# Rotary halves exchanged in the read instead of projected twice, and a retention norm summed with two products per head

## The reference, cut to what matters

```python
def apply_rope(t, cos, sin):                       # 64 channels: halves of 32
    t1, t2 = jnp.split(tf, 2, axis=-1)
    return jnp.concatenate([t1 * cos - t2 * sin, t1 * sin + t2 * cos], axis=-1)

def mla_mixer(h, cos, sin, w_in, q_norm, kv_norm, w_uq, w_ukv, w_o):
    c_q, c_kv, k_r = jnp.split(h @ w_in, [512, 768], axis=-1)      # 512, 256, 64
    q = (rms_norm(c_q, q_norm) @ w_uq).reshape(B, S, 8, 128 + 64)
    q_rope = apply_rope(q[..., 128:], cos, sin)
    kv = (rms_norm(c_kv, kv_norm) @ w_ukv).reshape(B, S, 8, 128 + 128)
    k_rope = apply_rope(k_r, cos, sin)
    ...                                            # causal attention, then @ w_o

def retention_mixer(h, w_in, out_g, w_out):        # 4 heads, keys 256, values 512
    ...
    ret = rms_norm_2(ret, out_g.reshape(4, 512))   # over the 512 values of a head
    y = ret * jax.nn.silu(g)
    return y @ w_out
```

## Time and profile before

| | |
|---|---|
| runs, us | 2784.96, 2791.34, 2791.89; median 2791.34 |
| profiled execution, us | 2785.44 |
| its span on the profile's clock, us | 2783.6 |
| TensorE busy | 2657.9 us, 95% |
| GpSimd busy | 1936.2 us, 70% |
| VectorE busy | 1084.8 us, 39% |
| mean granted TensorE clock | 0.976 of full |

### The profile page before, as it was taken

How to read it: one execution, slowest core, us unless ns; L and a number is a source line. 1 busy time by engine, 2 the same in 40 slices (tenths; PEclk the granted TensorE clock), 3 DMA queues, 4 the chain that set the end, 5 groups by cost and what they waited for, 6 DMA issues and landing times.

```text
span 2783.6 us, 33532 instructions
## 1 busy us (share of the span) xinstructions
PE 2657.9 (95%) x11988; PEld 2124.7 (76%) x11988; DVE 1084.8 (39%) x1871; ACT 735.2 (26%) x1188; POOL 1936.2 (70%) x1664
## 2 busy tenths in 40 slices
PE   6999899998999889999899999999999999899999
PEld 4766788886778668888756788888877877688887
DVE  6323411125666351112437553425531431452424
ACT  3333400113455340011344431202221121421211
POOL 5534688886666478888533388887958757688785
PEclk9999999999999999999989999999999999899999
DMA  5211233222222123223211133333313222233332
GB/s 151 69 38 58 69 101 106 91 94 73 76 60 76 40 82 106 91 93 103 61 46 46 30 91 97 100 92 91 106 47 110 71 74 76 63 104 97 100 91 76
DMA packets 297263, 225.80 MB, mean 81 GB/s; under 512 B 26979, under 2 KB 290124, under 8 KB 297036
## 3 DMA queue, kind: packets, MB, share of 16 engines
q1 hardware_dynamic: 294256, 219.21, 25.9%
q10 hardware_dynamic: 2908, 5.24, 0.5%
HBM read 222.32 MB, written 2.10 MB: 81 GB/s over the span
## 4 chain that ended last, share of the span: by engine, by line
PE 87%; DVE 5%; ACT 2%; issue 2%; POOL 1%; DVEq 1%; DMA 1%; ACTq 0%; SPq 0%; POOLq 0%
PE proj L547 26%; PE proj L549 26%; PE proj L548 26%; PE aux L1933 1%; PE aux L447 1%; PE aux L1853 1%; PE aux L1858 1%; PE aux L1774 1%; ACT L472 1%; POOL w_lo L1158 1%; PE proj L1715 1%; PE aux L1909 1%; PE proj L1714 1%; PE proj L741 1%; POOL w_hi L1153 0%
## 5 line engine op out<-in xcount | busy, mean ns | idle before, releaser
L547 PE MATMUL proj<-a_hi,w_hi 128*128 128x512 f32 x2104 | 841.7, 400 | 47.9 <-DVE a_lo L658 31.6
L549 PE MATMUL proj<-a_hi,w_lo 128*128 128x512 f32 x2104 | 825.1, 392 | 0.0
L548 PE MATMUL proj<-a_lo,w_hi 128*128 128x512 f32 x2104 | 824.6, 392 | 0.0
L1152 POOL TENSOR_TENSOR w_hi<-raw,small 128x512 fp32r<-128x512 f32 x375 | 393.2, 1049 | 593.9 <-PE proj L549 574.5
L1153 POOL TENSOR_TENSOR w_hi<-raw,small 128x512 fp32r<-128x512 f32 (+1 forms) x455 | 490.9, 1079 | 196.2 <-PE proj L549 194.2
L1158 POOL TENSOR_TENSOR w_lo<-raw,w_hi 128x512 fp32r<-128x512 f32 (+1 forms) x455 | 601.0, 1321 | 6.3
L1157 POOL TENSOR_TENSOR w_lo<-raw,w_hi 128x512 fp32r<-128x512 f32 x375 | 487.7, 1301 | 29.4
L547 PEld LDWEIGHTS proj<-a_hi,w_hi 128*128 128x128 f32 x2104 | 398.9, 190 | 140.8 <-issue 52.8
L547 PE MATMUL proj<-g_hi,w_hi 128*128 128x512 f32 x1216 | 478.0, 393 | 17.1 <-DVE g_lo L534 10.1
L548 PE MATMUL proj<-g_lo,w_hi 128*128 128x512 f32 x1216 | 475.3, 391 | 0.0
L549 PE MATMUL proj<-g_hi,w_lo 128*128 128x512 f32 x1216 | 475.2, 391 | 0.0
(11 more groups left out here) (255 smaller groups left out, 2226.5 us busy)
## 6 DMA issues: line engine op xcount, KB each, us to landing
raw<-in_mlp_w SPq DMA_DIRECT2D x64, 1024.0 KB, 5.3
raw<-in_f_w_up SPq DMA_DIRECT2D x88, 512.0 KB, 4.6
raw<-in_b_w_in SPq DMA_DIRECT2D x24, 1024.0 KB, 5.1
raw<-in_hgrn_w_in SPq DMA_DIRECT2D x32, 512.0 KB, 4.7
raw<-in_f_w_down SPq DMA_DIRECT2D x16, 1024.0 KB, 5.2
raw<-in_b_w_out SPq DMA_DIRECT2D x8, 1024.0 KB, 5.0
raw<-in_a_w_in SPq DMA_DIRECT2D x6, 1024.0 KB, 5.3
raw<-in_f_w_down SPq DMA_DIRECT2D x8, 768.0 KB, 4.4
```

The lines of the kernel that those rows point to most:

```text
L547: pe.matmul(psum[r][:], w_hi[r][:, w], xh, start=k == 0, stop=False)
L548: pe.matmul(psum[r][:], w_hi[r][:, w], xl, start=False, stop=False)
L549: last = pe.matmul(psum[r][:], w_lo[r][:, w], xh, start=False, stop=k == kc - 1)
L1152: pool.tensor_tensor(hi[:, 0:n], src[:, 0:n], nothing.to_broadcast([P, n, P]), ALU.subtract)
```

## The change

Two things change.

1. **Rotary parts.** The units with exchanged halves are gone: `st_mla_in` has seven units, and a pair of heads seven (`PAIR`). `rotate` multiplies the one bank by the cosine, and then, in four instructions on 32 partitions each, multiplies the partner's 32 partitions of the bank by the sine and writes them to the partner's place. Since seven doesn't go into four banks evenly, the loop over the two turns is written out as two stages, so the addresses are constants. All later units shift by five places in the bank order.
2. **The retention's norm.** Squares of blocks 0, 1 and 2 are added by VectorE (in PSUM bank `aux1`, then into the tile `ret_vT[0]`), and TensorE multiplies ones by that total and by the square of block 3, after all four output blocks.

```diff
-        st_mla_in = stage(1, [...] + [
-            Slab(DC, 2, lambda i: [(64 * r, 64, w_in[:, :, kr0:kr0 + 64]) for r in range(2)]
-                 + [(128 + 32 * r, 32, w_in[:, :, kr0 + 32 * (1 - r % 2):kr0 + 32 * (1 - r % 2) + 32]) for r in range(4)])])
+            Slab(DC, 1, lambda i: [(64 * r, 64, w_in[:, :, kr0:kr0 + 64]) for r in range(2)])])
...
-            p += [(384 + 64 * h + 32 * r, 32, uq[:, :, bass.ds(c0(h) + MLA_NOPE + 32 * (1 - r), 32)])
-                  for h in range(2) for r in range(2)]
...
-        st_mla = stage(MLA_HEADS // MLA_TURN, [
-            s for a in range(0, MLA_TURN, 2) for s in (
-                Slab(MLA_Q // P, 4, lambda i, a=a: uq_parts(i, a)),
+        st_mla = [stage(1, [
+            s for a in range(t, t + MLA_TURN, 2) for s in (
+                Slab(MLA_Q // P, 3, lambda i, a=a: uq_parts(a)),
+                plain(mla_w_ukv[0], kc=MLA_KV // P, width=2 * KVH, col=lambda i, a=a: a * KVH))])
+            for t in range(0, MLA_HEADS, MLA_TURN)]
+        PAIR = 7
...
+        class PairedNorm(Norm):
+            def square(self, act, src, c, i):
+                if c == 0:
+                    act.wait_ge(sq_used.sem, i * self.per + self.base)
+                if c == 3:
+                    act.wait_ge(sq_used.sem, i * self.per + self.base + 1)
+                act.activation(sq[c % 2] if c else self.running, src, ACT.Square).then_inc(sq_ready.sem, 1)
+            def add(self, dve, c, i):
+                dve.wait_ge(sq_ready.sem, i * self.per + self.base + c + 1)
+                if c == 2:
+                    dve.wait_ge(sq_used.sem, i * self.per + self.base + 1)
+                dve.tensor_tensor(self.running if c == 1 else self.total, self.running, sq[c % 2],
+                                  ALU.add).then_inc(sq_used.sem, 1)
+            def sum(self, pe, i):
+                pe.wait_ge(log_ready.sem, i * self.gper + self.gbase)
+                pe.wait_ge(sq_used.sem, i * self.per + self.base + 2)
+                pe.matmul(self.bank[:], ones[:], self.total, start=True, stop=False).then_inc(sq_used.sem, 1)
+                pe.wait_ge(sq_ready.sem, i * self.per + self.base + 4)
+                pe.matmul(self.bank[:], ones[:], sq[1], start=False, stop=True).then_inc(sq_used.sem, 1)
...
-                for k, table in ((0, rope_cos), (1, rope_sin)):
-                    bank = arrived(dve, st, j + k, i)
-                    dve.tensor_tensor(tmp[k], bank[:], table, ALU.mult).then_inc(*taken(st, j + k))
-                emptied(dve, st, j + 1, i)
+                bank = arrived(dve, st, j)
+                dve.tensor_tensor(tmp[0], bank[:], rope_cos, ALU.mult)
+                for r in range(0, P, MLA_ROPE // 2):
+                    here = slice(r, r + MLA_ROPE // 2)
+                    other = r ^ (MLA_ROPE // 2)
+                    last = dve.tensor_tensor(tmp[1][here, :], bank[other:other + MLA_ROPE // 2, :], rope_sin[here, :], ALU.mult)
+                last.then_inc(*taken(st, j))
+                emptied(dve, st, j)
                 dve.tensor_tensor(dst, tmp[0], tmp[1], ALU.add).then_inc(done.sem, 1)
...
+                dve.wait_ge(*ret_v_turned.at(2, h))
+                n_ret.add(dve, 1, h)
+                n_ret.add(dve, 2, h)
                 dve.wait_ge(*n_ret.ready(0, h))
```

More of the change, by code:

```diff
@@ L815, in program @@
         v_turned, v_ready = signal("v_turned", MLA_TURN), signal("v_ready", MLA_TURN)
-        V_AFTER = {6: 0, 8: 1, 14: 2, 15: 3}
+        V_AFTER = {5: 0, 7: 1, 12: 2, 13: 3}
         at_mla = Attention(MLA_TURN, MLA_HEADS // MLA_TURN, MLA_SCALE, [tile(acc, 4 + k) for k in range(3)] + [log_ms], sq)
@@ L1105, in program @@
         ret_o, ret_raw_ready, ret_y = signal("ret_o", RV), signal("ret_raw_ready", RV, credit=1), signal("ret_y", RV)
-        n_ret = Norm(RV, turns=RET_HEADS, size=RET_DV)
+        n_ret = PairedNorm(RET_HEADS, RET_DV, ret_vT[0])
         s_ret = Split(RV, RET_HEADS)
@@ L1204, in _, with mla_heads @@
                 s_c.round(act, tile(g_hi, c), c)
-            def mla_heads(i):
+            def mla_heads(st, i):
                 for a in range(2):
-                    for j, dst in ((0, qn[2 * a]), (1, qn[2 * a + 1]), (4, kn[2 * a]), (5, vT[0]), (6, kn[2 * a + 1]), (7, vT[1])):
-                        j += 8 * a
-                        bank = arrived(act, st_mla, j, i)
-                        act.copy(dst, bank[:]).then_inc(*taken(st_mla, j))
+                    for j, dst in ((0, qn[2 * a]), (1, qn[2 * a + 1]), (3, kn[2 * a]), (4, vT[0]), (5, kn[2 * a + 1]), (6, vT[1])):
+                        j += PAIR * a
+                        bank = arrived(act, st, j)
+                        act.copy(dst, bank[:]).then_inc(*taken(st, j))
                         if j in V_AFTER:
@@ L1216, in mla_heads @@
                 at_mla.act(act, i, lambda hh: tile(a_hi, i * MLA_TURN + hh))
-            turns(act, st_mla.turns, mla_heads)
+            for t, st in enumerate(st_mla):
+                mla_heads(st, t)
             out_mla.act(act)
@@ L1338, in ret_head @@
                     act.wait_ge(*ret_o.at(m, h))
-                    n_ret.square(act, aux[2 + m % 2][:], m, 0, h)
+                    n_ret.square(act, aux[2 + m % 2][:], m, h)
                     act.copy(ret_raw[m], aux[2 + m % 2][:]).then_inc(ret_raw_ready.sem, 1)
@@ L1685, in _ @@
             units_together(pe, st_mla_in, range(2), DC, a_hi, a_lo, 0, pre_mla.ready)
-            for j in range(2, 8):
+            for j in range(2, 7):
                 unit(pe, st_mla_in, j, DC, a_hi, a_lo)
@@ L1691, in _, with mla_heads @@
                         n.sum(pe, c)
-            def mla_heads(i):
-                for j in range(st_mla.per):
-                    a, q = divmod(j, 8)
-                    if q < 4:
-                        unit(pe, st_mla, j, MLA_Q // P, g_hi, g_lo, i, ready=s_c.low.at if j == 0 else None)
-                    else:
-                        unit(pe, st_mla, j, MLA_KV // P, g_hi, g_lo, i, k0=4,
-                             ready=(lambda k: s_c.low.at(4 + k)) if j == 4 else None)
+            def mla_heads(st, i):
+                for j in range(st.per):
+                    a, q = divmod(j, PAIR)
+                    if q < 3:
+                        unit(pe, st, j, MLA_Q // P, g_hi, g_lo, ready=s_c.low.at if j == 0 else None)
+                    else:
+                        unit(pe, st, j, MLA_KV // P, g_hi, g_lo, k0=4,
+                             ready=(lambda k: s_c.low.at(4 + k)) if j == 3 else None)
                     if j in V_AFTER:
                         hh = V_AFTER[j]
-                        emptied(pe, st_mla, 8 * (hh // 2) + 5 + 2 * (hh % 2), i)
+                        emptied(pe, st, PAIR * (hh // 2) + 4 + 2 * (hh % 2))
                         if hh >= 2:
@@ L1717, in mla_heads @@
                 at_mla.pe(pe, i, score, lambda hh, kb: vtok[hh][:, kb * P:kb * P + P])
-            turns(pe, st_mla.turns, mla_heads)
+            for t, st in enumerate(st_mla):
+                mla_heads(st, t)
             pe.wait_ge(tables_in, TABLES_IN)
@@ L1924, in ret_head @@
                 pe.wait_ge(*ret_v_ready.at(RV - 1, h))
-                for m in range(RV + 1):
-                    if m < RV:
-                        if m >= 2:
-                            pe.wait_ge(*ret_raw_ready.at(m - 2, h))
-                        for b in range(TB):
-                            if m == 0:
-                                pe.wait_ge(*ret_s_ready.at(b, h))
-                            e = b * RET_DV + m * P
-                            last = pe.matmul(aux[2 + m % 2][:, b * P:T], ret_vtok[:, e:e + P], ret_s[b][:, 0:T - b * P],
-                                             start=b == 0, stop=b == TB - 1, skip_group_check=True)
-                        last.then_inc(ret_o.sem, 1)
-                    if m >= 1:
-                        n_ret.sum(pe, m - 1, 0, h)
+                for m in range(RV):
+                    if m >= 2:
+                        pe.wait_ge(*ret_raw_ready.at(m - 2, h))
+                    for b in range(TB):
+                        if m == 0:
+                            pe.wait_ge(*ret_s_ready.at(b, h))
+                        e = b * RET_DV + m * P
+                        last = pe.matmul(aux[2 + m % 2][:, b * P:T], ret_vtok[:, e:e + P], ret_s[b][:, 0:T - b * P],
+                                         start=b == 0, stop=b == TB - 1, skip_group_check=True)
+                    last.then_inc(ret_o.sem, 1)
+                n_ret.sum(pe, h)
             def ret_out(st, j, i, h):
```

26 lines of the change are left out of this document (14 added, 12 removed).

## The result

| | before | after |
|---|---|---|
| runs, us | 5, 2784.96 to 2791.89 | 5, 2765.14 to 2773.08 |
| median, us | 2790.17 | 2771.18 |
| profiled execution, us | 2785.44 | 2771.18 |
| its span, us | 2783.6 | 2769.4 |
| mean granted clock | 0.976 | 0.974 |

The ratio of the times is 0.9932, with a 95% interval of 0.9917 to 0.9948: 19.0 us less by the medians. The forecast was 20.1 us less than the mean of 2788.4, that is 2768; the measured median is 3 us above it and inside the stated range of 2758 to 2778.

What follows compares the result with a forecast made beforehand. TensorE, busy 95% of the span, was taken to bound the kernel. 16.4 (latent attention) + 6.9 (retention) - 3.2 (new wait) = 20.1 us less than the mean of 2788.4, so 2768 us, range 2758 to 2778.

Steps and rivals of the forecast that it cites:

- the forecast's choice between 0.61 and 0.71 us: Pace of VectorE's narrow products in a rotation: 0.61 us back to back, 0.71 if each waits for the last; took 0.71.
- The work removed: Latent attention on TensorE: one unit of eight chunks (5.47 us) and four of four (10.92 us) go, together 16.4 us.
- GpSimd held nothing back: Latent attention: GpSimd's splits (12.4 us a pair) stay ahead of TensorE (13.6); rival that GpSimd becomes the bound, chance 0.04.
- The new wait: First pair's fourth unit: TensorE waits 3.2 us for the rotary keys' bank, which VectorE frees at 94.36; 2.8 without dependence.
- lower bound: Keys' bank wait: 2.0 us if VectorE's two low parts ahead, 2.14 us beside GpSimd, were done 0.8 us sooner.
- The query rotations: Heads' units: VectorE needs 3.7 us, bank wanted after 4.1 and a transposition; 0.4 us cover, no second wait or 0.2.
- The retention: Retention's norm: two products by ones fewer per head, 1.72 us each head, 6.9 us in all; VectorE's additions stay hidden.
- Written-out turns: Latent attention's loop over two turns written out: counted at nothing, since only a loop's branch is removed.
- the new wait costs the clock: Rival: TensorE's 3.2 us idle time lowers the clock behind it, losing 2 to 4 us; saving 17, 2771; chance 0.22.
- if the number of clock falls differs by more than one: Whole execution: a sign that would show the prediction wrong; one fall to 1.2 GHz was put at about 7 us.

Runs made afterwards that it cites:

- experiment 5: The changed kernel with two more narrow products in each rotation, ahead of the four; median 2768.82 us, ratio 0.9929.
- experiments 2 and 8: The kernel before with only the new retention norm (2782.53 us, ratio 0.9971), and with only the turns written out (2785.12 us, ratio 0.9984).
- experiment 2: The kernel before with only the retention's new norm; median 2782.53 us, ratio 0.9971.
- experiment 8: The kernel before with only the two turns of heads written out as two stages; median 2785.12 us, ratio 0.9984.
- experiments 4 to 6: The changed kernel with narrow products in one group (2777.53 us), with six narrow products (2768.82 us), and with one product by ones (2776.36 us).
- experiment 1: The changed kernel with the old norm, so only the rotary parts change; median 2778.80 us, ratio 0.9948.
- experiment 6: The changed kernel with one product by ones per head, VectorE adding block 3's square too; median 2776.36 us, ratio 0.9963.
- experiment 4: The changed kernel with all four narrow products of a rotation in one partition group; one execution, 2777.53 us.
- experiment 3: The changed kernel with the keys rotated before the last two latent blocks are normalized; median 2767.70 us, ratio 0.9924.

## Why the profiled pair differs by 14 us only

From the last sum over the latents to the attention's first product it was 42.67 us (82.11 to 124.78) and is 36.35 (82.79 to 119.14). In the second turn the heads' units took 36.42 us (171.98 to 208.40) and take 31.03 (157.52 to 188.55): 5.4 us less, two units of four chunks. By the start of the output units, the changed kernel is 20.5 us ahead (226.93 for 247.44); but 8.8 us of this are the first attention, which had a clock of 0.82 before and took 47.20 us, and takes 38.38 now. At the end it is ahead by 14.3 (2760.41 for 2774.68), although the retention gives 6.9 more. So between the output units and the retention (247.44 to 1567.04 before, 226.93 to 1559.65 after, the same 5820 products but for one record) it loses 13.1 us. Windows of equal work, from and to the same product in both kernels, show where. The columns are the window, its length, each engine's busy time, TensorE's granted clock (PEclk), DMA share and GB/s. Before:

```profile
core 0: us, PE busy (x) PEld busy (x) DVE busy (x) ACT busy (x) POOL busy (x), PEclk, DMA share, GB/s
...
661.91:737.53 75.62, 68.64 (x347) 55.36 (x347) 51.34 (x74) 40.61 (x54) 46.07 (x37) 0.98 0.20 56
...
919.14:951.04 31.90, 28.54 (x160) 22.42 (x160) 10.71 (x24) 11.14 (x14) 0.00 (x0) 0.95 0.00 1
...
1511.52:1567.04 55.52, 49.85 (x304) 38.16 (x305) 42.36 (x205) 41.18 (x111) 0.00 (x0) 0.96 0.05 19
1567.04:2774.68 1207.64, 1194.40 (x5190) 969.21 (x5191) 464.87 (x632) 242.68 (x347) 928.87 (x784) 0.99 0.28 86
```

After:

```profile
642.68:721.47 78.79, 72.25 (x347) 58.50 (x347) 50.73 (x74) 40.61 (x54) 45.63 (x38) 0.92 0.20 54
...
903.09:938.21 35.12, 32.94 (x160) 26.54 (x161) 10.69 (x24) 11.15 (x14) 0.00 (x0) 0.80 0.00 1
...
1500.61:1559.65 59.04, 51.38 (x305) 39.36 (x305) 44.90 (x210) 41.30 (x111) 0.00 (x0) 0.94 0.05 16
1559.65:2760.41 1200.76, 1187.36 (x5174) 965.42 (x5175) 470.62 (x640) 242.87 (x347) 929.22 (x784) 0.99 0.28 86
```

The first window holds 347 products in both kernels, the second 160; the change doesn't touch either. They take 3.2 us longer each, and the granted clock is 0.92 for 0.98 and 0.80 for 0.95. The fourth window starts at the retention and takes 6.9 us less at the same clock. So the clock fell in different places in the two executions, in stages that are the same. Over the whole span, the trace's record of the clock has 14 stretches at 1.2 GHz before, 134 us together, and 17 after, 147 us together.

**One stage lost time by another thing than chance.** The third window is the end of the third layer's sparse attention: 59.04 us for 55.52, 3.5 more. TensorE's idle time in it grew by 2.0 us (59.04 - 51.38 against 55.52 - 49.85); the rest goes with 3.4 us more at 1.2 GHz. Ahead of it VectorE picks the largest scores in three loops of 16 turns, one each for blocks of 256, 384 and 512 columns. The idle time ahead of the 16 instructions MAX8 of the last loop, before, after, and in experiment 5 that of the loop of 384 columns:

```profile
L1557 DVE MAX8 top<-F 128x8 f32<-128x512 f32 x16 | 11.1, 695 | 5.2 <-issue 5.1
...
L1593 DVE MAX8 top<-F 128x8 f32<-128x512 f32 x16 | 11.1, 695 | 8.8 <-issue 8.6
...
L1596 DVE MAX8 top<-F 128x8 f32<-128x384 f32 x16 | 9.0, 561 | 8.7 <-issue 8.6
```

After, nearly every turn of the last loop has 0.55 us of idle time ahead of it and not 0.34, although its instructions are the same and last the same. VectorE ends the loop 2.9 us behind TensorE's first product of the window, where it was 0.6 us ahead of it, and TensorE waits for it. In experiment 5's profile and in those of before and experiments 2 and 8, the clock doesn't fall behind this place; in the other seven it does. The last loop has 5.2 us in all three profiles of kernels with eight units per pair (before, experiments 2 and 8), and 8.7 or 8.8 us in seven of the eight with seven units. The eighth is experiment 5: there the loop of 384 columns is the slow one, and the window takes 55.53 us. So the loss comes with the rotary parts of the change, and an edit further ahead in VectorE's program moves it to another loop. Why a loop's turn gets slower is not shown; no experiment moved only the place of the loop.

All this makes a single pair of profiles a poor measure here. A better one: every execution is listed with its mean granted clock. Over the 125 executions of all kernels of this study for which it is listed, one straight line with a level for each kernel and one slope for all (least squares) leaves 1.7 us of scatter: 0.001 of mean clock is 2.29 us (2.17 to 2.41). The levels can then be compared **at the same clock**; this is the last column (95% interval of the fit). The executions come from three further chips and, for the changed kernel, the first result's five; a level for each chip as well moves the last column by 0.8 us at most.

| kernel | executions | mean us | mean clock | against before at the same clock, us |
|---|---|---|---|---|
| before | 54 | 2788.6 | 0.9752 | 0 |
| after | 12 | 2771.0 | 0.9742 | -19.7 ± 1.1 |
| rotary parts only | 9 | 2778.3 | 0.9737 | -13.7 ± 1.2 |
| retention's norm only | 12 | 2781.8 | 0.9754 | -6.3 ± 1.1 |
| keys rotated earlier | 13 | 2770.0 | 0.9732 | -23.2 ± 1.1 |
| six narrow products | 4 | 2768.4 | 0.9765 | -17.2 ± 1.7 |
| norm with one product | 10 | 2776.5 | 0.9733 | -16.4 ± 1.2 |
| turns written out only | 10 | 2784.0 | 0.9765 | -1.5 ± 1.2 |
| narrow products in one group | 1 | 2777.5 | 0.971 | -20.6 ± 3.4 |

A caution: where a kernel's own wait makes the clock fall, this column leaves that cost out.

## The experiments

**1. Only the rotary parts.** The changed kernel with the old norm.

```diff
-        n_ret = PairedNorm(RET_HEADS, RET_DV, ret_vT[0])
+        n_ret = Norm(RV, turns=RET_HEADS, size=RET_DV)
...
-                            n_ret.square(act, aux[2 + m % 2][:], m, h)
+                            n_ret.square(act, aux[2 + m % 2][:], m, 0, h)
```

> Only the rotary part of the change; the retention's norm is as in the kernel before. My account: 16.4 us of products gone, a wait of 2.9 us for the keys' bank, so 13.5 us less than before, and the retention's stretch as long as before. Rival, that the whole change works through something else (fewer clock falls, other bank order): a saving far from 13.5, or a shorter retention too.

Median 2778.80 us (2769.53 to 2785.98, 9 executions), before beside it 2792.13: ratio 0.9948 [0.993, 0.9967]. At the same clock 13.7 ± 1.2 us less. Its fourth unit:

```profile
93.91 0.47 PE L545 MATMUL proj<-g_hi,w_hi 128*128 128x512 f32 x1 [2.71 <-issue]
94.21 0.40 PE L546 MATMUL proj<-g_lo,w_hi 128*128 128x512 f32 x1
```

The same wait of 2.71 us, but here the products behind it keep 0.39 us: the clock stays. The wait comes from the rotary parts alone, and what the clock does behind it is not settled by the wait's length.

**2. Only the retention's norm.** The kernel before with the new norm, so the units with exchanged halves are there.

```diff
-        n_ret = Norm(RV, turns=RET_HEADS, size=RET_DV)
+        n_ret = PairedNorm(RET_HEADS, RET_DV, ret_vT[0])
```

> Only the retention's norm is changed; the rotary parts are as in the kernel before. My account: two products by ones of 0.86 us fewer per head, on the chain in all four heads: 6.9 us less than before, and the chain of a head with blocks in one piece of 8.6 us. Rival, that TensorE's gain is given back where heads 0 to 2 have other work in between: 1.7 us less (only the fourth head).

Median 2782.53 us (2770.45 to 2796.45, 12): ratio 0.9971 [0.9952, 0.9991]; at the same clock 6.3 ± 1.1 less. The heads' units of the second turn take 36.43 us as before, and the retention's chain has the pieces of the changed kernel. The two parts add up: 13.7 + 6.3 = 20.0 against 19.7 for both.

**3. The keys rotated earlier.** VectorE rotates the keys before it normalizes the last two latent blocks; their bank is full long before.

```diff
-            normed_c(n_ckv, "mla_kv", 4, 2)
...
-            dve.wait_ge(*s_c.low.at(5))
+            dve.wait_ge(*s_c.low.at(3))
             rotate(st_mla_in, 6, k_rope, k_rope_ready)
             dve.wait_ge(*k_rope_ready.at(0))
+            normed_c(n_ckv, "mla_kv", 4, 2)
+            dve.wait_ge(*s_c.low.at(5))
```

> The changed kernel with one move on VectorE: the keys are rotated before the key and value latents are normalized, while VectorE waits for their root, instead of after. My account: the bank of the keys is free at about 87.4 instead of 94.6, TensorE's idle time of 2.7 us at the fourth unit is gone, and the kernel is 2.9 us faster than the changed one (about 22 us under the kernel before). Rival: the rotation delays the latents' last low parts, so TensorE waits for these instead, by about as much, and nothing is gained. By times: the latents start at 87.9 in the changed kernel, the rotation would take from 83.8 to 88.1, so a delay of 0.3 us against a need at 91.8.

Median 2767.70 us (2757.20 to 2779.93, 6): ratio 0.9924 [0.9899, 0.9948]. VectorE:

```profile
83.84 0.69 DVE L1459 TENSOR_TENSOR F<-proj,F 128x512 f32<-128x512 f32 x1
84.54 2.79 DVE L1463 TENSOR_TENSOR F<-proj,F 32x512 f32<-32x512 f32 x4
87.37 1.22 DVE L1466 TENSOR_TENSOR F<-F 128x512 f32<-128x512 f32 x1
...
90.06 2.14 DVE L564 TENSOR_TENSOR g_lo<-F,g_hi 128x512 fp32r<-128x512 f32 x2
```

The rotation now fills VectorE's idle time ahead of the latents (the changed kernel has 4.05 us of it ahead of 87.85, where it waits for ScalarE). The low parts are done at 92.20, 1.2 us later than in the changed kernel. TensorE doesn't notice: it asks for the first of the two ahead of the product at 91.80, when it is done, and for the second a chunk later, at 92.48, 0.3 us after its end. The fourth unit starts without idle time:

```profile
91.80 0.39 PE L577 MATMUL proj<-g_hi,w_hi 128*128 128x512 f32 x1
92.03 0.39 PE L578 MATMUL proj<-g_lo,w_hi 128*128 128x512 f32 x1
```

From the last sum over the latents to the attention it takes 31.79 us, not 36.35: 4.6 us less, of which 2.9 are the wait and 1.6 what the clock behind it cost in that profile. I ran it once more, since the intervals of the two kernels overlap:

> The changed kernel with the keys rotated ahead of the last two latent blocks, once more. Theory: at the same granted clock it is 3 to 4.5 us faster than the changed kernel (2.9 us of wait, and what a clock fall behind that wait costs), so some 23 to 24 us less than before, and its fourth unit has no idle time. Rival: the first result was chance, and it lies with the changed kernel, 19.7 us below before.

Median 2772.11 us (2763.52 to 2778.89, 7), ratio 0.9938 [0.9906, 0.9969], and 31.75 us for the same stretch. The medians alone don't tell it from the changed kernel. At the same clock it is 3.5 ± 1.3 us faster, which agrees with the wait of 2.9; in that column it is the fastest version measured.

**4. All four narrow products in one group.** This leaves out the exchange of halves and three quarters of the sine terms: four products read partitions 0 to 31 and write them in four tiles.

```diff
-                for r in range(0, P, MLA_ROPE // 2):
-                    here = slice(r, r + MLA_ROPE // 2)
-                    other = r ^ (MLA_ROPE // 2)
-                    last = dve.tensor_tensor(tmp[1][here, :], bank[other:other + MLA_ROPE // 2, :], rope_sin[here, :], ALU.mult)
+                here = slice(0, MLA_ROPE // 2)
+                for to in (tmp[1], dst, sq[0], sq[1]):
+                    last = dve.tensor_tensor(to[here, :], bank[here, :], rope_sin[here, :], ALU.mult)
```

> The changed kernel, but the four narrow products of a rotation all read partitions 0 to 31 and write partitions 0 to 31 of four different tiles, so no instruction starts in another group than the one ahead of it. This leaves out the exchange of halves and three quarters of the sine terms. If the longer pace (0.70 us) comes from the change of group, the four start 0.61 us apart here and take 2.5 us instead of 2.79, and the wait at the fourth unit is 0.3 us shorter (2.4). Rival: the pace belongs to narrow products as such, then 2.79 us and 2.7 us stay.

One execution, 2777.53 us. VectorE's keys' rotation, and TensorE's fourth unit:

```profile
91.51 0.69 DVE L1460 TENSOR_TENSOR F<-proj,F 128x512 f32<-128x512 f32 x1
92.11 2.46 DVE L1463 TENSOR_TENSOR F<-proj,F 32x512 f32<-32x512 f32 x4
```

```profile
94.68 0.47 PE L577 MATMUL proj<-g_hi,w_hi 128*128 128x512 f32 x1 [2.29 <-POOL w_lo L1188]
```

The four last 2.46 us, so they start 0.59 us apart; the first starts 0.60 us after the product on 128 partitions, where it was 0.71. TensorE's idle time is 2.29 instead of 2.71 us. So the forecast's choice between 0.61 and 0.71 us was a real one, and 0.4 us of the wait is the change of partition group; the rest stays with five products at the shorter pace. The profile names GpSimd as the releaser, but its `w_lo` was done at 93.89; VectorE's last narrow product ends at 94.57, 0.1 us ahead of TensorE's start, as in the changed kernel.

**5. Six narrow products.** Two more in each rotation, into a tile that the addition overwrites.

```diff
                 dve.tensor_tensor(tmp[0], bank[:], rope_cos, ALU.mult)
+                for r in (0, 32):
+                    here = slice(r, r + 32)
+                    dve.tensor_tensor(dst[here, :], bank[here, :], rope_sin[here, :], ALU.mult)
```

> The changed kernel with two more narrow products in each rotation (into the tile that the sum then overwrites), ahead of the four. Each rotation gives its bank back 1.4 us later. By the account of cover (0.4 us and the transposition of some 0.4 us ahead of the unit that wants the bank): the keys' wait grows by 1.4 us, and each of the four query rotations makes TensorE wait 0.4 to 0.8 us where it did not wait: 3.0 to 4.6 us slower than the changed kernel. Rival, that the query rotations are covered much more widely: 1.4 us slower only.

Median 2768.82 us (2763.92 to 2771.84, 4 executions at a high mean clock): ratio 0.9929 [0.9902, 0.9956]. At the same clock it is 2.5 ± 1.9 us slower than the changed kernel.

```profile
91.67 0.69 DVE L1460 TENSOR_TENSOR F<-proj,F 128x512 f32<-128x512 f32 x1
92.27 1.36 DVE L1463 TENSOR_TENSOR F<-proj,F 32x512 f32<-32x512 f32 x2
93.65 2.79 DVE L1467 TENSOR_TENSOR F<-proj,F 32x512 f32<-32x512 f32 x4
```

```profile
96.54 0.76 PE L577 MATMUL proj<-g_hi,w_hi 128*128 128x512 f32 x1 [3.99 <-issue]
...
118.95 0.47 PE L577 MATMUL proj<-g_hi,w_hi 128*128 128x512 f32 x1 [0.51 <-DVE F L1467]
...
174.48 0.47 PE L577 MATMUL proj<-g_hi,w_hi 128*128 128x512 f32 x1 [0.44 <-DVE F L1467]
```

The first narrow product stays in the group of the one ahead of it and starts 0.60 us after it; the others change group. The keys' wait grows by 1.3 us to 3.99, and three of the four query rotations now hold a bank, with idle times of 0.51, 0.44 and 0.51 us (the third, in the second pair of turn 2, not shown). The modelled ends of products make these look short: the heads' units of the second turn take 32.44 us (161.06 to 193.50) and not 31.03, so a wait costs 0.7 us. Together 1.3 + 3 x 0.7 = 3.4 us. A rotation that lasts 1.3 us longer made TensorE 0.7 us late, so the queries' cover was 0.6 us. The 2.0 us of the selection loop are not lost in this profile, so the difference from the changed kernel should be 1.4 us, within 2.5 ± 1.9.

**6. The norm with one product.** VectorE adds the fourth square too, and TensorE makes one product by ones.

```diff
-                pe.wait_ge(sq_used.sem, i * self.per + self.base + 2)
-                pe.matmul(self.bank[:], ones[:], self.total, start=True, stop=False).then_inc(sq_used.sem, 1)
-                pe.wait_ge(sq_ready.sem, i * self.per + self.base + 4)
-                pe.matmul(self.bank[:], ones[:], sq[1], start=False, stop=True).then_inc(sq_used.sem, 1)
+                pe.wait_ge(sq_used.sem, i * self.per + self.base + 3)
+                pe.matmul(self.bank[:], ones[:], self.total, start=True, stop=True).then_inc(sq_used.sem, 1)
...
+                n_ret.add(dve, 3, h)
```

> The changed kernel with one product by ones per head instead of two: VectorE adds the square of block 3 too. One product of 0.86 us fewer, but the product now waits for block 3's square (0.12 + 0.60 us after the block) and VectorE's addition (0.69 us and two handovers), some 1.5 us after block 3, so it ends at 2.5 us behind the block instead of 1.9: 0.6 us slower per head, 2.4 us in all, and TensorE idle 1.5 us in each head. Rival, that fewer products are always better: 3.4 us faster.

Median 2776.36 us (2765.49 to 2789.89, 10): ratio 0.9963 [0.9944, 0.9982]. The chain in head 1:

```profile
2043.28 8.64 PE aux L1971 x32
...
2052.02 0.61 ACT F L528
...
2052.65 0.70 DVE F L535
...
2053.40 1.12 PE aux L542 x2
```

The product that goes was the one that TensorE made while ScalarE squared block 3. Now TensorE waits for the square and for the addition. From the blocks' end to the sum's end it is 2.60 us, against 1.89: 0.7 us a head, some 2.8 us in all. The kernel is 3.3 ± 1.4 us slower than the changed kernel at the same clock.

**7. The changed kernel again**, on the chip of experiments 4 to 6, for its clock.

> The changed kernel once more. The latent attention and the retention should last what they lasted in the first profile (from the last sum of the latents to the first attention 36.4 us; 6.9 us less than before in the retention), within 0.3 us where the clock is the same. The stages between them that the change doesn't touch should differ from the first profile only where the granted clock falls at other places, by some us each, and the time should fall between 2765 and 2773. Rival, that the change itself costs time in these stages (written-out turns, another bank order): then the same stages are longer than before by the same amounts again.

Median 2774.12 us (2760.53 to 2777.89, 7): ratio 0.9953 [0.9933, 0.9973]. Its profiled execution was the shortest, 2760.53 us with a clock of 0.979. Its fourth unit:

```profile
93.42 0.47 PE L577 MATMUL proj<-g_hi,w_hi 128*128 128x512 f32 x1 [2.71 <-issue]
93.72 0.39 PE L578 MATMUL proj<-g_lo,w_hi 128*128 128x512 f32 x1
...
94.52 0.63 PE L578 MATMUL proj<-g_lo,w_hi 128*128 128x512 f32 x1
```

The same wait, and 0.8 us behind it the products begin to last 0.63 us. The fall behind the keys' wait came in the changed kernel's two profiles and in experiment 6, not in experiment 1 with the same wait, nor in experiment 4 with 2.29 us; it came in experiment 5 with 3.99 us, and lasted longer there.

The expectation's rival, that the change costs time in stages that it doesn't touch, can be answered here, since the clock was high as in before's profile. From the output units to the window of the sparse attention it takes 1264.2 us (225.64 to 1489.87), before 1264.1 (247.44 to 1511.52). That window then takes 59.04 us again (1489.87 to 1548.91), for 55.52 before. So the rival holds for the selection loop and nowhere else.

**8. Only the turns written out.** The kernel before, its two turns of heads as two stages with constant addresses, and nothing else.

```diff
-        st_mla = stage(MLA_HEADS // MLA_TURN, [
-            s for a in range(0, MLA_TURN, 2) for s in (
+        st_mla = [stage(1, [
+            s for a in range(t, t + MLA_TURN, 2) for s in (
...
-            turns(pe, st_mla.turns, mla_heads)
+            for t, st in enumerate(st_mla):
+                mla_heads(st, t)
```

> The kernel before, with the two turns of the latent attention written out as two stages, and nothing else: the units with exchanged halves stay and the norm is the old one. It does alone what the prediction counted at nothing. Theory: each kernel with written-out turns had an attention of 38.4 us where the looped ones had 39.0 to 39.3 us at the same clock, with TensorE's idle time behind the attention 1.4 us in place of 2.1 to 2.3 us; so the written-out turns alone give 0.7 us per attention, some 1.3 us in all, and the time at the same granted clock is 1 to 1.5 us shorter. Rival: the shorter attention comes with the changed bank order of seven units; then it stays at 39.0 us here, with 2.1 us of idle time, and the time is unchanged.

Median 2785.12 us (2776.55 to 2794.23, 10), before beside it 2786.49: ratio 0.9984 [0.9961, 1.0008]. At the same clock 1.5 ± 1.2 us less. TensorE's first product behind each of the two attentions:

```profile
165.28 0.51 PE L548 MATMUL proj<-g_hi,w_hi 128*128 128x512 f32 x1 [1.40 <-DVE a_lo L771]
...
240.16 0.50 PE L548 MATMUL proj<-a_hi,w_hi 128*128 128x512 f32 x1 [1.40 <-DVE a_lo L771]
```

Before, the same products had 2.30 and 2.07 us of idle time. The changed kernel has 1.40 us:

```profile
157.52 0.50 PE L577 MATMUL proj<-g_hi,w_hi 128*128 128x512 f32 x1 [1.40 <-DVE a_lo L800]
```

Both attentions take 38.4 us (126.91 to 165.28, 201.78 to 240.16). The loop's two at a full clock, in experiment 2, took 39.29 (123.99 to 163.28) and 39.02 us (199.71 to 238.73), and before's second one 39.04 (208.40 to 247.44). So the written-out turns give 0.9 us in the first turn and 0.7 in the second, 1.6 together, and the bank order has no part in it.

## Why the prediction was right

- **The work removed.** Forecast 16.4 us. The first turn's stretch is 42.67 - 36.35 = 6.3 us shorter; with the wait (2.9) and the clock behind it (1.6) this makes 10.8, forecast 5.47 + 2 x 2.73 = 10.9. The second turn gives 5.4. Experiment 1 fits, though its sum needs two terms that the forecast had at nothing: 16.4 - 2.9 + 1.6 (turns) - 2.0 (selection loop) = 13.1, against 13.7 ± 1.2 at the same clock. GpSimd held nothing back.
- **The new wait.** Forecast 3.2 us, measured 2.9 (2.71 recorded as idle). The pace of 0.71 us was right (0.70). VectorE started the rotation 8.33 us after the last sum (82.79 to 91.12) and not 8.73 as in the earlier trace rows, since the two low parts ahead of it took 1.71 and not 2.14 us; this is the reason that the "lower bound" was given for, and half of it came. TensorE started 0.1 us after the rotation's end, which the forecast had left out. The Trainium skill's rule ("VectorE: DVE Perf Modes", section "Two Vector instructions with no wait between them"), that a change of partition group makes an instruction begin only when the ones ahead have finished, decides between the two paces: the trace agrees, 0.70 us with a change and 0.59 to 0.60 without (experiments 4 and 5).
- **The query rotations.** Forecast: covered by 0.4 us and the transposition. No wait in the changed kernel, and experiment 5 measures the cover at 0.6 us.
- **The retention.** Forecast 6.9 us, with 0.17 us of waiting for the last square left in each sum. Window 1559.65 on: 6.9 us. Experiment 2: 6.3 ± 1.1. The second addition ended 0.7 us before the blocks, so the additions are hidden, and experiment 6 shows that two products are better than one.
- **Written-out turns: mis-sized.** The forecast's "written-out turns I count at nothing too, since they remove only a loop's branch" was wrong by 1.6 us (0.9 + 0.7; experiment 8). The row was there: TensorE idled 2.30 and 2.07 us at the loop's end before.
- **Stages not touched: left out.** The forecast gives nothing for them. The slower turns of VectorE's selection loop cost 3.5 us, 2.0 of idle time and 1.5 with the clock behind it. No row of before could have told; its cause is open.
- **The clock.** The rival "the new wait costs the clock", chance 0.22, came in part: in the window behind the wait the clock is 0.66, while the attention of the second turn has 1.00:

```profile
94.00:99.00 5.00, 4.28 (x12) 3.40 (x13) 4.84 (x8) 0.59 (x1) 1.23 (x2) 0.66 0.36 105
...
188.00:227.00 39.00, 37.04 (x185) 22.44 (x185) 20.63 (x84) 19.50 (x54) 12.89 (x12) 1.00 0.16 55
```

It cost 1.6 us there in three of the four profiles with exactly this wait, a little under the 2 to 4 us given. That cost belongs in the sum, not beside it. The forecast's own sign of being wrong, "if the number of clock falls differs by more than one", did occur: 14 stretches at the low clock before and 17 after. The long one in the first attention went, and shorter ones came in other stages. The time stayed inside the range all the same.

With the measured wait and these three terms the sum would have been 16.4 + 6.9 - 2.9 - 1.6 + 1.6 - 3.5 = 16.9 us. The means of the table differ by 17.6 (2788.6 and 2771.0), the medians of the first result by 19.0. At the same clock it is 16.4 + 6.9 - 2.9 + 1.6 - 2.0 = 20.0, against 19.7 ± 1.1. There the two terms that the clock costs drop out. So the terms that the forecast had were right, and that its 20.1 came so near the first result is in part luck: it left out 1.6 and 3.5 us of loss and 1.6 us of gain, and the rest is the scatter between executions.

What decides these falls is open. Equal waits in equal surroundings gave both outcomes, and no experiment changed the clock alone. That keys rotated earlier save the 1.6 us too is seen in that stretch of two profiles (31.79 and 31.75 us), not in the mean clock of whole executions (0.9732 against 0.9742).

## What to carry to other kernels

When units leave a rotation of banks, look up who empties the bank that now comes round first: here it was an engine still busy with something that nobody needed yet, and the cure was to give it the two jobs in the other order. Replace a product on the bounding engine by work on an idle one only as far as that work ends before the last input is there; the last product by ones was covering a wait, and the additional addition stood on the path. And where time scatters by ten microseconds and the granted clock is listed with each execution, compare the kernels at the same clock before reading a difference of a few microseconds, and then compare windows of equal work in stages that weren't touched: here one of them had become 3.5 us longer.

## What the runs showed of the hardware

- One straight line in the mean granted clock explains nearly all scatter: executions of before lie between 2776.76 and 2803.72 us, at clocks of 0.980 to 0.969, and 1.7 us are left around the line. A mean lower by 0.001 is, by estimate, 2770 x 0.002 = 5.5 us spent at 1.2 instead of 2.4 GHz, and it cost 2.29 us, 0.41 us for each. Dense products say nearly the same: at the low clock they start 0.43 us apart and not 0.23, which loses 0.47 us in each.
- One fall in an attention costs 7.9 to 9.5 us (47.2 for before's first attention against 39.0; 46.2 and 47.9 in experiments against 38.4). It came in the first (before, experiments 4 and 6), the second (experiments 1, 5 and the repeat of 3) or neither. Experiment 3's kernel had it in one of its two profiles and not in the other.
- A VectorE product on 32 partitions costs what one on 128 does (0.68 us for 512 columns); changing the partition group adds 0.10 us to the pace.
- A loop's turn on TensorE cost 0.9 us of idle time where the loop goes on (2.31 in experiment 2 against 1.40) and 0.7 where it ends (2.07 against 1.40), at a place where the engine waited for VectorE anyway.
- A loop of the same VectorE instructions had turns 0.21 us longer in one kernel than in another (0.55 against 0.34 us of idle time), in a stage that the edit didn't touch.
